# Stores behind row loads, a count of its own for the first norm, and row work moved into the first two experts

## The chip, the cores and the metric

The kernel runs on one core of one Trainium2 chip. The metric is device time in microseconds (us) of one launch; several executions are made and their median is compared. Engines: TensorE (PE in the views; PEld its weight loads), VectorE (DVE), ScalarE (ACT), GpSimd (POOL) and SyncE (SP), each with an instruction stream of its own. They are kept in order by semaphores: `then_inc` raises one, `wait_ge` holds an engine until it has a value. [...]

## The reference, cut to what matters

One transformer-like layer is applied to 128 prompt rows and to 256 sample rows (to which position rows are added), 1024 wide. A mixer (scans of three kinds, among them matrix-valued head states) is followed by a residual layer norm, a routed mixture of 16 experts and a second layer norm. The head states after the prompt are outputs too.

```python
y, finals = _mixer(x * (1 + sc1) + sh1, init, ...)
x = _layer_norm(ALPHA * x + g1 * y, ln1_g, ln1_b)
h = x * (1 + sc2) + sh2
scores = softmax(h @ w_router)            # 16 experts in 4 groups; best group, top 2 of it
act = silu(h @ w_gate[e]) * (h @ w_up[e]) * combine[e]
f = sum_e act @ w_down[e]
x = _layer_norm(ALPHA * x + g2 * f, ln2_g, ln2_b)
```

## The kernel before

The 384 rows are three row tiles (`NT` = 3) of 128 partitions. All matrices are held in float32; for a product, each operand is split in a rounded high part (ScalarE, `w_hi`) and a low part (VectorE subtracts, `w_lo`), and TensorE adds three products of them (`mm3`). A weight piece of 2 MB is split in four "units" of 128x1024; four unit buffers go round. SyncE streams the weight pieces.

**The mixer's end and the first norm.** TensorE projects with `w_out` in three parts; the third part is given out half row by half row, tile by tile (`y_ready`). In between `turned_rows(i)` transposes tile i's normed input and multiplies it with the router's weights. VectorE waits for the rows it needs, adds the position rows (L2048), then waits for the counts `ln_in` (eight loads: ln1_g, ln1_b, ln2_g, ln2_b, b_router, tri, desc16, iota) and `g_in` (four), folds the norm's gain and bias into the modulation rows (L2099 to L2102), and goes through `mixed_half(i, half)` (scale by g1, add to the residual, statistics; L2057 to L2059), `centred_rows`, `scaled_rows`, `router_logits`, `selection` and, at i == 2, `residual(0)`, which makes the row that the second norm will add to (L2091 to L2093: one small instruction and two of 1024 columns). Each uses `step`, which waits for the instruction's own end.

All loads of these rows are issued by POOL, in this order: after the last mask of the matrix heads it waits for `cfin_sb`, stores the final states `C_FIN` (512 KB) and `n_fin` (4 KB, in pieces of 4 bytes), loads the modulation rows (g1; then sc2 and sh2), the residual rows and the position rows, and then ln1_g, ln1_b, ln2_g, ln2_b, b_router, tri, desc16 and iota. Later come the indirect stores of the routed rows.

**Routing.** VectorE ranks the scores, TensorE counts ranks with `tri` (it too waits for `ln_in`), `slots_of(b)` makes selection matrices, and `selected(b)` multiplies the first two experts' rows out.

**The experts.** One expert has twelve units: up 4 to 7, the next expert's gate 8, 9, down 10 to 13, the next expert's gate 14, 15. TensorE runs 4 to 7, 8, the transposes of the activation (L1601), 9, 10 to 13, 14, 15, then turns the rows of the expert after next. VectorE makes the low parts in the same order, with `tokens_lo` before 8, `gated` (L2213) after 9 and `act_lo` (L2217) before 11. ScalarE makes the high parts, at most four units ahead of TensorE, with silu before 7. Before `expert(0)` VectorE runs `last_rows()`: residual(1), residual(2), `last_sel` (three instructions) and the picks (six small ones). TensorE transposes `last_sel` in its own `last_rows()` (L1571) between `expert(0)` and `expert(1)`. ScalarE's `last_rows()` stands behind its `expert(1)` and before `expert(2)`:

```python
def last_rows():                                   # ScalarE
    act.wait_ge(S["last_sel_T"], 1)
    act.activation(last_T, ps[:, 7, 0:T]..., ACT.Identity)           # L1046
    act.wait_ge(S["pick_ready"], 1)
    for c in range(2):
        for i in range(2):
            act.activation(pick_diag[:, c, i, :], ident, ...)       # L1050
...
expert(base + 1, p0, 1, p0 if base else None)
over = None
if base == 0:
    last_rows()
```

Of the kernel before, what the change touches and what calls it, by code (L numbers as in the profile page):

```python
# [29 lines left out]
ALU = mybir.AluOpType  # L30
# [3 lines left out]
P = 128  # L34
# [6 lines left out]
T = SEQ + LAT  # L41
NT = T // P
# [216 lines left out]
def build(nc, a, outs):  # L259
    with ExitStack() as ctx:  # L260
# [145 lines left out]
        def moe(off, n):  # L406
            return arena[:, off:off + n]
# [46 lines left out]
        ln_stats = early("ln_stats", 36).rearrange("p (i x) -> p i x", i=NT)  # L454
        ln_mv = early("ln_mv", 6).rearrange("p (i x) -> p i x", i=NT)
        ln_rstd, ln_rstd_a = [early(x, 3) for x in ("ln_rstd", "ln_rstd_a")]
        first_row = early("first_row", 16)
        SEL = [early(f"slot_sel{b}", 384).rearrange("p (i r) -> p i r", i=NT) for b in range(2)]

        kept = colsA  # L460
# [11 lines left out]
        row_sq = kept[:, 49:52]  # L472
        row_rstd = kept[:, 52:55]
        pick_diag = moe(6800, 512).rearrange("p (c i t) -> p c i t", c=2, i=2)
        last_sel = moe(7312, 384).rearrange("p (i r) -> p i r", i=NT)
# [187 lines left out]
        def _(pool):  # L663
# [53 lines left out]

            pool.wait_ge(S["cfin_sb"], 16)
            pool.dma_start(outs[4][0, 0].rearrange("d h p e -> p (d h) e"), C_FIN).then_inc(S["out_C"], 16)
            pool.dma_start(outs[5][0, 0].rearrange("d h p -> p (d h)"), n_fin, allow_slow_non_contiguous=True).then_inc(S["out_small"], 16)  # L720

            sem, value = TAKEN[("chan", "mo", C - 1)]
# [18 lines left out]
            for v, name in enumerate(("ln1_g", "ln1_b", "ln2_g", "ln2_b")):  # L741
                pool.dma_start(ln_b[:, v, :], a[name][0].partition_broadcast(P)).then_inc(S["ln_in"], 16)
            pool.dma_start(b_router, a["b_router"].partition_broadcast(P)).then_inc(S["ln_in"], 16)
            pool.dma_start(tri, a["consts"][:, 128:256]).then_inc(S["ln_in"], 16)
            pool.dma_start(desc16, a["consts"][:, 384:400]).then_inc(S["ln_in"], 16)
            pool.dma_start(iota, a["consts"][:, 256:384]).then_inc(S["ln_in"], 16)
            pool.wait_ge(S["zeroed_first"], 16 * ZERO_FIRST)
            pool.wait_ge(S["in_zeroed"], 16 * (12 - ZERO_FIRST))
# [422 lines left out]
        def _(pe):  # L1171
# [378 lines left out]
            pe.wait_ge(S["mask_ready"], 1)  # L1550
            pe.wait_ge(S["ln_in"], 16 * 8)
            mm(ps[:, 1, 0:64], tri, mask, True, False)
# [78 lines left out]
            def expert_pass(base):  # L1631
# [10 lines left out]
                if base:  # L1642
                    turn(base + 1, 1, p0)
                expert(base, 0, p0, True, base > 0)
                if base == 0:
                    last_rows()
                expert(base + 1, 1, p0, True)
                with pe.Fori(1, NPAIR - 1) as i:
# [35 lines left out]
        def _(dve):  # L1684
# [409 lines left out]

            dve.wait_ge(S["ln_in"], 16 * 8)
            dve.wait_ge(S["g_in"], 16 * 4)
            step(ts(first_row, desc16, -float(P), float(16 * P), ALU.mult, ALU.add))
            for s in range(2):
# [10 lines left out]
            centred_rows(0)  # L2109
            scaled_rows(0)  # L2110
            for i in range(1, NT):
                mixed_half(i, 0)
                router_logits(i - 1)
                selection(i - 1)
                if i == 2:
                    residual(0)
                mixed_half(i, 1)
                centred_rows(i)
                if i < NT - 1:
                    scaled_rows(i)  # L2120
# [61 lines left out]

            def last_rows():

                for i in (1, 2):
                    residual(i)
                for i in range(NT):
                    step(ts(last_sel[:, i, :], iota, last_rank[:, i:i + 1], last_w[:, i:i + 1], ALU.is_equal, ALU.mult), "last_sel")
                step(ts(in_last, rows, float((NE - 1) * P), None, ALU.is_ge))
                step(stt(in_last, rows, float(NE * P), in_last, ALU.is_lt, ALU.mult))  # L2190
                step(stt(rows, in_last, -float(P), rows, ALU.mult, ALU.add))
                step(dve.tensor_copy(row_e, rows))
                step(ts(in_last, in_last, -1.0, 1.0, ALU.mult, ALU.add))
                step(tt(pick_e.rearrange("p c i -> p (c i)"), pick_w.rearrange("p c i -> p (c i)"), in_last, ALU.mult), "pick_ready")
# [23 lines left out]

            def expert(n, b, bank=0):

# [9 lines left out]
                for q in range(1, 4):  # L2230
                    lo(n, 10 + q, down, q)
                for q in (2, 3):
                    lo(n, GATE_NEXT[q], gate, q)

            def expert_pass(base):
# [6 lines left out]
                lo(base, 3, gate, 3)  # L2242
                if base == 0:
                    last_rows()
                expert(base, 0, 0 if base else 5)
                over = dve.value_load(over_i[0:1, 0:1], min_val=0, max_val=T) if base == 0 else None
                expert(base + 1, 1)
                with dve.Fori(1, NPAIR - 1) as i:
                    for b in range(2):
                        expert(2 * i + (base + b), b)  # L2250
                expert(base + NE - 2, 0)
                n = base + NE - 1
# [98 lines left out]
```

## Time and profile before

| | |
|---|---|
| median of 3 runs | 752.32 us (751.73 to 752.75) |
| profiled execution, its own time | 752.86 us |
| its span, first to last instruction | 751.0 us |
| TensorE busy | 686.0 us, 91% |
| VectorE busy | 575.5 us, 77% |
| ScalarE busy | 433.0 us, 58% |
| mean granted TensorE clock | 0.961 |

Times in the rows are us from the span's start. The profiled execution lies 1.86 us over its span and 0.54 us over the median. The granted clock is a share of the full 2.4 GHz. In square brackets after an instruction stands the time its engine was idle before it and which instruction released it; L12 is line 12 of the kernel.

### The profile page before, as it was taken

To read this page: it belongs to the slowest core of one execution; us is meant where nothing else is said; L and a number is where in the kernel's file an instruction comes from. 1 tells how busy PE (TensorE), PEld (TensorE's weight loads), DVE (VectorE), ACT (ScalarE), POOL (GpSimd) and SP (SyncE) were. 2 spreads that over 40 slices of the span, in tenths; PEclk is the share of its full clock that TensorE was granted. 3 is DMA by queue.
4 is the path that set the end of the run, shared out by engine and by line. 5 is a ranking of instruction groups with operands and counts; after the bars stand their busy time and mean duration, and the time that the engine had idled before them with its cause. 6 is when DMAs were issued, how large, how long until landed. Compare 5 with 4: busy or idle time off the path is not lost.

```text
span 751.0 us, 12527 instructions
## 1 busy us (share of the span) xinstructions
PE 686.0 (91%) x4818; PEld 552.4 (74%) x4818; DVE 575.5 (77%) x838; ACT 433.0 (58%) x604; POOL 57.1 (8%) x88
## 2 busy tenths in 40 slices
PE   3599999999899999999794899999999999999881
PEld 2488988898689889944364878888888888888640
DVE  2649998788992457651767998998999998999765
ACT  1646966273223546530034378888888888888721
POOL 2060000000011001240000400000000000000210
PEclk9799999999999999999976999999999999999996
DMA  9999496466747898899403999999999999999242
GB/s 336 372 247 354 156 387 239 141 220 201 275 139 278 293 394 308 297 171 399 164 0 130 399 339 391 398 399 399 400 399 399 399 400 398 400 398 388 86 143 84
DMA packets 91508, 220.06 MB, mean 293 GB/s; under 512 B 3336, under 2 KB 3632, under 8 KB 91456
## 3 DMA queue, kind: packets, MB, share of 16 engines
q1 hardware_dynamic: 85200, 200.29, 72.1%
q0 software_dynamic: 5840, 18.94, 8.3%
q8 instruction: 33, 0.54, 0.3%
q10 hardware_dynamic: 415, 0.14, 0.1%
q14 instruction: 20, 0.16, 0.1%
HBM read 179.99 MB, written 39.36 MB: 292 GB/s over the span
## 4 chain that ended last, share of the span: by engine, by line
PE 69%; DVE 18%; DMA 6%; ACT 3%; issue 2%; SPq 1%; POOL 1%; DVEq 0%; ACTq 0%
PE ps L1173 66%; DMA iota<-in_consts 4%; DMA ring<-in_w_in 3%; PE ps L1582 2%; DVE w_lo L1745 2%; DVE arena L1900 1%; DVE arena L1899 1%; PE ps L1601 1%; DVE arena L1845 1%; DVE w_lo L2199 1%; ACT w_hi L829 1%; DVE arena L2093 1%; DVE arena L2290 1%; DVE arena L2092 1%; DVE arena L2292 1%
## 5 line engine op out<-in xcount | busy, mean ns | idle before, releaser
L2199 DVE TENSOR_TENSOR w_lo<-arena,w_hi 128x1024 fp32r<-128x1024 f32 x96 | 115.0, 1221 | 9.4 <-ACT w_hi L1057 8.3
L2199 DVE TENSOR_TENSOR w_lo<-ring,w_hi 128x1024 fp32r<-128x1024 f32 x92 | 109.9, 1221 | 8.8 <-ACT w_hi L1057 7.8
L1057 ACT ACTIVATE w_hi<-arena 128x1024 fp32r<-128x1024 f32 x96 | 101.2, 1064 | 17.0 <-PE ps L1173 16.8
L1173 PE MATMUL ps<-h_hi,w_lo 128*128 128x384 f32 x288 | 101.8, 354 | 7.4 <-DVE w_lo L1745 5.2
L1057 ACT ACTIVATE w_hi<-ring 128x1024 fp32r<-128x1024 f32 x92 | 96.8, 1063 | 19.8 <-PE ps L1173 19.5
L1173 PE MATMUL ps<-w_hi,slot_tokens_lo 128*128 128x512 f32 x256 | 103.1, 403 | 2.1 <-DVE w_lo L2199 2.1
L1173 PE MATMUL ps<-w_hi,slot_tokens_hi 128*128 128x512 f32 x256 | 101.0, 394 | 0.0
L1173 PE MATMUL ps<-w_lo,slot_tokens_hi 128*128 128x512 f32 x256 | 100.5, 393 | 0.0
L1173 PE MATMUL ps<-h_lo,w_hi 128*128 128x384 f32 x288 | 97.3, 338 | 0.0
L1173 PE MATMUL ps<-h_hi,w_hi 128*128 128x384 f32 x288 | 97.3, 338 | 0.0
L1745 DVE TENSOR_TENSOR w_lo<-ring,w_hi 128x1024 fp32r<-128x1024 f32 x44 | 53.7, 1225 | 23.6 <-ACT w_hi L829 22.6
L1173 PE MATMUL ps<-ring,arena 128*128 128x512 f32 x144 | 65.9, 616 | 0.4 <-DVE arena L1771 0.4
L829 ACT ACTIVATE w_hi<-ring 128x1024 fp32r<-128x1024 f32 x44 | 46.1, 1052 | 31.1 <-PE ps L1173 29.9
L1173 PEld LDWEIGHTS ps<-h_hi,w_lo 128*128 128x128 f32 x288 | 54.9, 191 | 12.3 <-issue 9.0
L1173 PE MATMUL ps<-arena 128*32 128x32 f32 (+5 forms) x1528 | 56.3, 220 | 4.1 <-DVE arena L1984 1.4
L1173 PEld LDWEIGHTS ps<-w_hi,slot_tokens_lo 128*128 128x128 f32 x256 | 48.6, 190 | 11.7 <-DVE w_lo L2199 2.5
L1173 PEld LDWEIGHTS ps<-w_hi,slot_tokens_hi 128*128 128x128 f32 x256 | 48.4, 189 | 10.4
L905 ACT ACTIVATE arena<-ps,small 128x384 f32<-128x384 f32 x32 | 18.5, 579 | 64.9 <-PE ps L1173 64.8
L1173 PEld LDWEIGHTS ps<-w_lo,slot_tokens_hi 128*128 128x128 f32 x256 | 48.6, 190 | 9.3
L1173 PEld LDWEIGHTS ps<-h_lo,w_hi 128*128 128x128 f32 x288 | 55.0, 191 | 0.6
L1173 PEld LDWEIGHTS ps<-h_hi,w_hi 128*128 128x128 f32 x288 | 54.8, 190 | 0.0
L1173 PEld LDWEIGHTS ps<-arena 128*32 128x32 f32 (+3 forms) x1528 | 44.4, 122 | 13.4 <-issue 5.7
(362 smaller groups left out, 1118.7 us busy)
## 6 DMA issues: line engine op xcount, KB each, us to landing
slot_rows<-arena SPq DMA_DIRECT2D x12, 2048.0 KB, 18.3
ring<-in_w_in SPq DMA_DIRECT2D x11, 2048.0 KB, 10.4
ring<-in_w_ada SPq DMA_DIRECT2D x10, 2048.0 KB, 9.0
ring<-in_w_up SPq DMA_DIRECT2D x8, 2048.0 KB, 15.0
ring<-in_w_down SPq DMA_DIRECT2D x8, 2048.0 KB, 11.2
arena<-in_w_gate SPq DMA_DIRECT2D x8, 2048.0 KB, 15.5
arena<-in_w_down SPq DMA_DIRECT2D x8, 2048.0 KB, 11.9
arena<-in_w_up SPq DMA_DIRECT2D x8, 2048.0 KB, 15.1
```

The source lines that it names most:

```text
L829: act.activation(part_unit(w_hi, u % 4, col), raw_unit(p % NSLOT, u % 4, col), ACT.Copy).then_inc(S["hi_ready"], 1)
L905: act.activation(chunk(dst_of[g], c), bank[:, 0:T], ACT.Gelu_apprx_tanh if g == "rg" else ACT.Identity, bias=bias).then_inc(S["z_taken"], 1)
L1057: act.activation(w_hi[:, at_ % 4, :], raw[:, q * QUARTER:(q + 1) * QUARTER], ACT.Copy).then_inc(S["hi_ready"], 1)
L1173: return pe.matmul(out, lhsT, rhs, start=start, stop=stop, skip_group_check=open_)
L1582: last = pe.transpose(ps[:, half, k * P:(k + 1) * P], XG[b][:, (4 * half + k) * P:(4 * half + k + 1) * P], ident)
L1601: last = pe.transpose(ps[:, 2, k * P:(k + 1) * P], AC[:, k * P:(k + 1) * P], ident)
L1745: tt(lo, raw, hi.bitcast(F32), ALU.subtract).then_inc(S["lo_dve"], 1)
L1845: step(dve.tensor_tensor_scan(hv, av, uv, init, ALU.mult, ALU.add))
L1899: step(tt(qh[right_q], qh[right_q], first.broadcast_to(shape), ALU.mult))
L1900: step(tt(kh[1 - right_q], kh[1 - right_q], last.broadcast_to(shape), ALU.mult))
L2092: step(stt(X1[:, i, :], X1[:, i, :], mean(i), gain, ALU.subtract, ALU.mult))
L2199: tt(w_lo[:, at_ % 4, :], raw[:, q * QUARTER:(q + 1) * QUARTER], w_hi[:, at_ % 4, :].bitcast(F32), ALU.subtract).then_inc(S["lo_dve"], 1)
```

## The change

- POOL: the wait for `cfin_sb` and the stores of `C_FIN` and `n_fin` move from ahead of the modulation rows to behind the load of iota.
- The loads of ln1_g and ln1_b are counted on `g_in` instead of `ln_in`. VectorE waits for `g_in` (six loads) ahead of the folding of gains, and for `ln_in` (now six) behind `scaled_rows(0)`, where `first_row` is now made. TensorE's wait for `ln_in` has the new count.
- `residual(0)` runs at i == 1 instead of i == 2.
- VectorE's `last_rows()` ahead of `expert(0)` is gone. `residual(1)` and `last_slots()` (the three `last_sel`) stand inside expert 0, and `residual(2)` and `picks()` inside expert 1, each behind unit 13 and ahead of unit 14. `value_load` of the overflow count moves behind the loop of experts.
- TensorE's `last_rows()` moves from behind `expert(0)` to behind `expert(1)`. ScalarE's stream is unchanged.
- `ln_mv`, `ln_rstd` and `ln_rstd_a` get places in `kept`, since they are now used inside the experts.

```diff
--- before.py
+++ after.py
@@ -452,8 +452,6 @@
         gain_c, bias_c = [early(x, 16).rearrange("p (k s) -> p k s", s=2) for x in ("gain_cols", "bias_cols")]
         least = early("least_win", 16)
         ln_stats = early("ln_stats", 36).rearrange("p (i x) -> p i x", i=NT)
-        ln_mv = early("ln_mv", 6).rearrange("p (i x) -> p i x", i=NT)
-        ln_rstd, ln_rstd_a = [early(x, 3) for x in ("ln_rstd", "ln_rstd_a")]
         first_row = early("first_row", 16)
         SEL = [early(f"slot_sel{b}", 384).rearrange("p (i r) -> p i r", i=NT) for b in range(2)]
 
@@ -471,6 +469,8 @@
         row_mean = kept[:, 46:49]
         row_sq = kept[:, 49:52]
         row_rstd = kept[:, 52:55]
+        ln_rstd, ln_rstd_a = kept[:, 55:58], kept[:, 58:61]
+        ln_mv = kept[:, 61:67].rearrange("p (i x) -> p i x", i=NT)
         pick_diag = moe(6800, 512).rearrange("p (c i t) -> p c i t", c=2, i=2)
         last_sel = moe(7312, 384).rearrange("p (i r) -> p i r", i=NT)
         last_T = moe(7696, 384).rearrange("p (i t) -> p i t", i=NT)
@@ -715,10 +715,6 @@
                                              pattern=[[0, nb], [sgn, P]], channel_multiplier=-sgn)
                     ins.then_inc(S["p_mask"], 1)
 
-            pool.wait_ge(S["cfin_sb"], 16)
-            pool.dma_start(outs[4][0, 0].rearrange("d h p e -> p (d h) e"), C_FIN).then_inc(S["out_C"], 16)
-            pool.dma_start(outs[5][0, 0].rearrange("d h p -> p (d h)"), n_fin, allow_slow_non_contiguous=True).then_inc(S["out_small"], 16)
-
             sem, value = TAKEN[("chan", "mo", C - 1)]
             pool.wait_ge(S[sem], value)
             pool.wait_ge(S["mod_stored"], 16)
@@ -739,11 +735,14 @@
             pool.dma_start(pos2, a["pos"].rearrange("(i p) d -> p i d", p=P)).then_inc(S["x2_in"], 16)
             pool.wait_ge(S["out_S"], 16)
             for v, name in enumerate(("ln1_g", "ln1_b", "ln2_g", "ln2_b")):
-                pool.dma_start(ln_b[:, v, :], a[name][0].partition_broadcast(P)).then_inc(S["ln_in"], 16)
+                pool.dma_start(ln_b[:, v, :], a[name][0].partition_broadcast(P)).then_inc(S["g_in" if v < 2 else "ln_in"], 16)
             pool.dma_start(b_router, a["b_router"].partition_broadcast(P)).then_inc(S["ln_in"], 16)
             pool.dma_start(tri, a["consts"][:, 128:256]).then_inc(S["ln_in"], 16)
             pool.dma_start(desc16, a["consts"][:, 384:400]).then_inc(S["ln_in"], 16)
             pool.dma_start(iota, a["consts"][:, 256:384]).then_inc(S["ln_in"], 16)
+            pool.wait_ge(S["cfin_sb"], 16)
+            pool.dma_start(outs[4][0, 0].rearrange("d h p e -> p (d h) e"), C_FIN).then_inc(S["out_C"], 16)
+            pool.dma_start(outs[5][0, 0].rearrange("d h p -> p (d h)"), n_fin, allow_slow_non_contiguous=True).then_inc(S["out_small"], 16)
             pool.wait_ge(S["zeroed_first"], 16 * ZERO_FIRST)
             pool.wait_ge(S["in_zeroed"], 16 * (12 - ZERO_FIRST))
             pool.wait_ge(S["route_ready"], 1)
@@ -1548,7 +1547,7 @@
             turned_rows(NT - 1)
 
             pe.wait_ge(S["mask_ready"], 1)
-            pe.wait_ge(S["ln_in"], 16 * 8)
+            pe.wait_ge(S["ln_in"], 16 * 6)
             mm(ps[:, 1, 0:64], tri, mask, True, False)
             for j in range(NT):
                 n = NT - j
@@ -1642,9 +1641,9 @@
                 if base:
                     turn(base + 1, 1, p0)
                 expert(base, 0, p0, True, base > 0)
+                expert(base + 1, 1, p0, True)
                 if base == 0:
                     last_rows()
-                expert(base + 1, 1, p0, True)
                 with pe.Fori(1, NPAIR - 1) as i:
                     for b in range(2):
                         expert(2 * i + (base + b), b, i + p0, True)
@@ -2092,9 +2091,7 @@
                 step(stt(X1[:, i, :], X1[:, i, :], mean(i), gain, ALU.subtract, ALU.mult))
                 step(stt(X1[:, i, :], X1[:, i, :], ln_rstd_a[:, i:i + 1], bias, ALU.mult, ALU.add))
 
-            dve.wait_ge(S["ln_in"], 16 * 8)
-            dve.wait_ge(S["g_in"], 16 * 4)
-            step(ts(first_row, desc16, -float(P), float(16 * P), ALU.mult, ALU.add))
+            dve.wait_ge(S["g_in"], 16 * 6)
             for s in range(2):
                 step(tt(H2[:, 0, :], bias, sc2_b[s], ALU.mult))
                 step(tt(sh2_b[s], sh2_b[s], H2[:, 0, :], ALU.add))
@@ -2108,11 +2105,13 @@
 
             centred_rows(0)
             scaled_rows(0)
+            dve.wait_ge(S["ln_in"], 16 * 6)
+            step(ts(first_row, desc16, -float(P), float(16 * P), ALU.mult, ALU.add))
             for i in range(1, NT):
                 mixed_half(i, 0)
                 router_logits(i - 1)
                 selection(i - 1)
-                if i == 2:
+                if i == 1:
                     residual(0)
                 mixed_half(i, 1)
                 centred_rows(i)
@@ -2180,12 +2179,12 @@
             step(tt(last_w, last_w, both_w, ALU.mult))
             slots_of(1)
 
-            def last_rows():
-
-                for i in (1, 2):
-                    residual(i)
+            def last_slots():
+
                 for i in range(NT):
                     step(ts(last_sel[:, i, :], iota, last_rank[:, i:i + 1], last_w[:, i:i + 1], ALU.is_equal, ALU.mult), "last_sel")
+            def picks():
+
                 step(ts(in_last, rows, float((NE - 1) * P), None, ALU.is_ge))
                 step(stt(in_last, rows, float(NE * P), in_last, ALU.is_lt, ALU.mult))
                 step(stt(rows, in_last, -float(P), rows, ALU.mult, ALU.add))
@@ -2216,7 +2215,7 @@
                 dve.wait_ge(S["act_T_sb"], n + 1)
                 tt(ACL, ps[:, 2, :].rearrange("p (k j) -> p k j", k=C), ACH.bitcast(F32), ALU.subtract).then_inc(S["act_lo"], 1)
 
-            def expert(n, b, bank=0):
+            def expert(n, b, bank=0, rows_of=None):
 
                 up, down, gate = expert_slot(1, b), expert_slot(2, b), expert_slot(0, 1 - b)
                 for q in range(4):
@@ -2229,6 +2228,12 @@
                 act_lo(n)
                 for q in range(1, 4):
                     lo(n, 10 + q, down, q)
+                if rows_of is not None:
+                    residual(rows_of)
+                if rows_of == 1:
+                    last_slots()
+                if rows_of == 2:
+                    picks()
                 for q in (2, 3):
                     lo(n, GATE_NEXT[q], gate, q)
 
@@ -2240,14 +2245,12 @@
                 lo(base, 2, gate, 2)
                 tokens_lo(base, 0, (1,))
                 lo(base, 3, gate, 3)
-                if base == 0:
-                    last_rows()
-                expert(base, 0, 0 if base else 5)
-                over = dve.value_load(over_i[0:1, 0:1], min_val=0, max_val=T) if base == 0 else None
-                expert(base + 1, 1)
+                expert(base, 0, 0 if base else 5, None if base else 1)
+                expert(base + 1, 1, 0, None if base else 2)
                 with dve.Fori(1, NPAIR - 1) as i:
                     for b in range(2):
                         expert(2 * i + (base + b), b)
+                over = dve.value_load(over_i[0:1, 0:1], min_val=0, max_val=T) if base == 0 else None
                 expert(base + NE - 2, 0)
                 n = base + NE - 1
                 up, down = expert_slot(1, 1), expert_slot(2, 1)
```

## Rows read from the trace of the kernel before

**Rows 1.** The page: chain by engine; costliest group (busy us, mean ns | idle).

```profile
PE 69%; DVE 18%; DMA 6%; ACT 3%; issue 2%; SPq 1%; POOL 1%; DVEq 0%; ACTq 0%
...
L2199 DVE TENSOR_TENSOR w_lo<-arena,w_hi 128x1024 fp32r<-128x1024 f32 x96 | 115.0, 1221 | 9.4 <-ACT w_hi L1057 8.3
```

**Rows 2.** The chain that ended last, in order of time: start, us, what.

```profile
333.95 27.17 DMA iota<-in_consts
...
397.65 0.70 DVE arena L2057
...
442.55 8.52 PE ps L1173 x36
...
460.96 8.52 PE ps L1173 x36
...
479.12 8.51 PE ps L1173 x36
```

**Rows 3.** Timeline of TensorE, 300 to 452: start, us, engine, line, operation, shapes.

```profile
328.36 34.50 PE L1173 MATMUL ps<-ring,arena 128*128 128x512 f32 x80
...
362.86 7.08 PE L1173 MATMUL ps<-ring,arena 128*128 128x512 f32 x16
...
388.71 1.04 PE L1529 MATMUL ps<-small,arena 128*128 128x128 f32 x8
...
391.80 3.68 PE L1173 MATMUL ps<-ring,arena 128*128 128x512 f32 x8
...
431.98 0.50 PE L1173 MATMUL ps<-w_hi,slot_tokens_lo 128*128 128x512 f32 x1 [2.10 <-DVE w_lo L2199]
...
440.53 0.60 PE L1601 MATMUL ps<-small,arena 128*128 128x128 f32 x4
...
451.77 0.49 PE L1571 MATMUL ps<-small,arena 128*128 128x128 f32 x3
```

**Rows 4.** Timeline of VectorE, 315 to 470.

```profile
353.73 2.29 DVE L2048 TENSOR_TENSOR arena<-arena 128x2048 f32<-128x2048 f32 x1 [20.69 <-DMA arena<-in_pos]
...
361.53 1.23 DVE L2099 TENSOR_TENSOR arena<-arena 128x1024 f32<-128x1024 f32 x1
...
369.81 0.69 DVE L2057 TENSOR_TENSOR arena<-ps,gain_rows 128x512 f32<-128x512 f32 x1
...
372.25 0.69 DVE L2057 TENSOR_TENSOR arena<-ps,gain_rows 128x512 f32<-128x512 f32 x1
...
385.55 0.69 DVE L2057 TENSOR_TENSOR arena<-ps,gain_rows 128x512 f32<-128x512 f32 x1 [4.07 <-PE ps L1173]
...
422.68 0.15 DVE L2091 TENSOR_SCALAR ln_rstd_a<-ln_rstd 128x1 f32<-128x1 f32 x1
...
428.33 1.11 DVE L2188 TENSOR_SCALAR arena<-iota,small 128x128 f32<-128x128 f32 x3
...
430.70 4.63 DVE L2199 TENSOR_TENSOR w_lo<-ring,w_hi 128x1024 fp32r<-128x1024 f32 x4
...
445.81 4.87 DVE L2199 TENSOR_TENSOR w_lo<-arena,w_hi 128x1024 fp32r<-128x1024 f32 x4
```

**Rows 5.** Timeline of ScalarE, 300 to 492.

```profile
431.43 1.05 ACT L1057 ACTIVATE w_hi<-ring 128x1024 fp32r<-128x1024 f32 x1
...
464.98 0.47 ACT L1046 ACTIVATE arena<-ps 128x384 f32<-128x384 f32 x1
...
466.52 2.94 ACT L1057 ACTIVATE w_hi<-ring 128x1024 fp32r<-128x1024 f32 x3
```

**Rows 6.** Stretch: PE, PEld, DVE, ACT, POOL busy; granted clock; DMA share; GB/s.

```profile
431.95:435.64 3.69, 3.66 (x10) 2.87 (x11) 3.69 (x4) 2.48 (x4) 0.00 (x0) 0.56 0.80 224
```

**Rows 7.** DMA: a stretch, columns as above; two issues, us to landing.

```profile
322.00:334.00 12.00, 12.00 (x32) 5.47 (x31) 7.87 (x20) 4.25 (x4) 5.68 (x11) 1.00 0.90 107
...
out<-small POOLq DMA_DIRECT2D x1, 4.0 KB, 15.3
...
arena<-in_ln_b POOLq DMA_DIRECT2D x1, 512.0 KB, 26.6
```

## Prediction, made before the changed kernel ran

> **What bounds the kernel now.** I read the chain of waits by engine first: TensorE holds 69% of it and VectorE 18% [rows 1], so an edit pays only where one of these two is last. Then the same chain in order of time. Two places answer to the change. The load of iota stands in it for 27.17 us, from 333.95 to 361.12 [rows 2]: that is the eight-load count at the head of the first norm. The second is the start of the experts: expert 0's up weights are multiplied from 431.98, after a wait of 2.10 us for VectorE [rows 3], and each expert then gives one "down" start, at 442.55, 460.96 and 479.12 [rows 2]. That is 18.16 us an expert. I call these starts D0, D1 and D2; they are my clock for the second half.
>
> TensorE does not wait while the load is awaited: 80 matmuls of the output projection take 34.50 us and the next 16, 7.08 us, so it is busy until 369.94 [rows 3]. VectorE finishes adding the position rows at 356.02, sits still, and prepares the gains from 361.53 to 369.81, 8.28 us [rows 4]. Its sums of row tile 0 then come too late for TensorE, whose next projections come too late for VectorE: it waits 4.07 us for them before 385.55 [rows 4].
>
> **Part 1, the first norm.** VectorE now waits for ln1_g and ln1_b alone. ln1_b was issued at 330.79 and took 26.6 us [rows 7], so it was there at 357.4; the 512 KB store of C_FIN and the store of n_fin (4-byte pieces) no longer lie ahead of it in POOL's queue. The six loads of the modulation rows, which POOL issued behind them, go out up to 3 us sooner too, and the position rows, whose addition ended at 356.02 [rows 4], come earlier with them. How much earlier it lands no row tells directly. From 322 to 334 the DMA engines were 90% busy and moved only 107 GB/s, and n_fin landed 15.3 us after its issue [rows 7]. If those two stores are what clogs them, the rows land about ten us earlier.
>
> By the Trainium skill ("DMA: Bandwidth & Descriptors", Anatomy of one DMA, SWDGE path) bytes cost their size over 436 GB/s, so that C_FIN would be worth only an estimated 1.2 us; the last landing would be 356.2, and the sum below would come out half a us longer. The 107 GB/s speak against it as the whole cost.
>
> The first half row of tile 0 needs the projection's first output (362.86), the second half row its second (362.86 plus half of 7.08, so 366.4) [rows 3]. With the gains ready by 362.9 (preparation begun by 354.6, which needs the position rows added by then) the first half starts at 362.86 and, 2.44 us long (369.81 to 372.25 [rows 4]), ends before the second output. A preparation begun as late as 355.5 loses nothing, since the second half starts with that output anyway. I take 366.45. From this half row (372.25) to the last tile's second half row (397.65) lie 25.40 us, of which 4.07 are the wait [rows 2, 4]. The instructions between stay the same (residual(0) only moves one tile up; first_row, 0.2 us, joins them): 21.5 us. TensorE keeps up: free at 369.94, turned rows and logits of a tile 3.1 us (388.71 to 391.80), two projections 7.1 us, thus 380.1, again 3.1 and 3.5: its last output stands at 386.8 [rows 3]. So the last half row starts at 388.0 instead of 397.65: **9.65 us gained**. Lower bound: ln1_b as before, at 357.5, gives 365.8, 368.2, 389.7: 7.9 us. Upper: the last output itself, 10.8 us. ln_in and tri, iota now have until 371 and 398, ten us and more beyond their landing. The C_FIN store is now issued at about 334.5, behind iota; SyncE's wait for it stands before expert 1's gate weights, which go out at about 400 (with h2_ready, 410 less the 9.65), and POOL's own next work, the indirect stores, comes later still. So I price it at nothing; 60 us late, it would hold those weights back.
>
> The new places of ln_mv and ln_rstd change no duration; I price them at nothing.
>
> **Part 2, expert 0.** Before, VectorE does residual(1), residual(2), last_sel and the picks in one piece from 422.68 to 430.70, 8.02 us, and only then unit 4 [rows 4]. TensorE waits for it until 431.98 [rows 3] and then runs 3.69 us at a granted clock of 0.56 [rows 6], that is mostly at 1.2 GHz instead of 2.4, which costs 3.69 x 0.44 = 1.6 us. With this piece gone the next things are late: ScalarE writes unit 7's high part only from 431.43, after its table load [rows 5], so VectorE's unit 7, a subtraction of 1.22 us [rows 1], ends at 433.7, the tokens' low halves at 434.9, unit 8 at 436.1, unit 9 and the gating product at 437.85. The transposes follow, and from their start to D0 it is 440.53 to 442.55, 2.02 us [rows 2, 3]. D0 = 439.9: **2.65 us gained**, not the 3.85 of wait and clock. Bounds: 1.6 (if the small waits now drop the clock) and 3.85.
>
> **Part 3, the two blocks.** After unit 13 of expert 0 VectorE now does residual(1) and last_sel, 8.02 halved: by 428.33 the two residuals had taken 5.65, so a residual is 2.82; last_sel is 1.15, the picks 1.22 [rows 4]. The blocks are 3.97 and 4.05 us. Before, unit 14 is begun by VectorE at 445.81, D0 + 3.26 [rows 4]. Now it ends at D0 + 3.26 + 3.97 + 1.22 + 0.05 = D0 + 8.5. TensorE wants it when its 24 down matmuls are through, D0 + 5.6 (36 matmuls take 8.52 [rows 2]). It stands still 2.9 us in expert 0 and, by the same sum, 3.0 in expert 1. Neither is short beside the 2.1 us before 431.98, after which the clock fell [rows 3, 6]: 1.6 us more each. Bounds for each clock term: 0 and 1.6.
>
> **Part 4, last_rows of TensorE behind expert 1.** ScalarE's place for it has not moved: after the high parts of expert 1, before expert 2. Before, TensorE's three transposes were at 451.77 [rows 3], 13 us ahead of ScalarE, which copies at 464.98 and goes on to expert 2's high parts at 466.52 without a wait, 1.54 us [rows 5]. Now the transposes start 9.22 us after the down start (442.55 to 451.77 [rows 2, 3]) plus the 3.0 of the block. Queued behind ScalarE's wait is unit 4 of expert 2, and TensorE and VectorE both wait for it. From the transposes' start: 0.55 to ScalarE, 1.54, high part 1.06, low part 1.22, handovers 0.1: 4.5, of which 0.25 is the transposes' own: **4.2 us** idle. Then all four buffers are empty and ScalarE and VectorE feed expert 2 as they go, with silu, the token copies and the out rows in between; as in part 2, unit 8 and the gating product come late, 1.3 us in all (bounds 0 and 2). Here the slow clock hides inside the same waits, so it costs about nothing more. VectorE's register load, now behind the loop, I price at nothing: it waits for no other engine there.
>
> **Sum.** Experts: -2.65 + 2.9 + 1.6 + 3.0 + 1.6 + 4.2 + 1.3 = +11.95. Norm: -9.65. Net +2.3 us. The profiled execution took 752.86 us with a span of 751.0, 1.86 around it, and lies 0.54 over the median, so 755.2 for it and **754.6** for the median. Behind D2 nothing is left over: each engine finds its old distance again, at TensorE's pace.
>
> **Rivals.** (a) The clock holds in one of the two idles (+0.7, 753.0) or in both (-0.9, 751.4). For: the handover gaps of an ordinary expert leave it at 1.0; against: 2.1 us sufficed before. (b) Rows do not land earlier, and the change does in part 1 only half of what it says: +1.75, 756.3. For: the queue's other seven loads stay; against: 107 GB/s. (c) Faster: VectorE's slack hides the two blocks. It decides at unit 14 of expert 0: a block of up to 5.6 - 3.26 - 1.28 = 1.1 us would be free, one of 3.97 is not. The price is 2.9 + 3.0 + 3.2, and the time 745.5. For: twelve low parts in sequence take some 14 us (four take 4.63 [rows 4]), which, with 2.6 us of small ones, leaves a good us of an expert's 18.16 free; against: that is all they leave. (d) Faster by less: the clock also holds at tile 2 of the norm and in both idles; some 0.8 more than (a), 750.6.
>
> **Chances and range.** Forecast 0.50, (a) 0.19 for one and 0.11 for both, (b) 0.08, (c) 0.05, (d) 0.07. This kernel's measurement tells 0.2%, 1.5 us, from nothing. Slower: the forecast less 0.03 for its lower edge, and (b): 0.55. Same: (a) and that 0.03, 0.33. Faster: (c) and (d), 0.12. The range runs from (d) to (b), 750.8 to 756.4.
>
> **What would show it.** Right: the last half row's L2057 about ten us before its old place; unit 4 right behind unit 3; TensorE idle for 3 us before unit 14 of experts 0 and 1, released by VectorE, with a clock near 0.5 behind it; ScalarE's L1046 waiting some 7 us for TensorE's transposes, and TensorE waiting 4 us before expert 2. Wrong: no hole before unit 14, or a hole of ScalarE under 4 us, or VectorE still waiting in the norm.

## The result and the profile after

The changed kernel takes 755.45 us (median of 7 runs, 753.81 to 756.17) against 751.73 us for the kernel before (7 runs, 748.08 to 753.61): a ratio of 1.0049, 95% interval 1.0026 to 1.0071. It is slower by 3.7 us, half a percent, with an interval of 2.0 to 5.3. The profiled execution took 754.52 us with a span of 752.7, at a mean granted clock of 0.963. In this kernel most line numbers are lower by one: L1172 is L1173 of before, L2056 is L2057.

The chain by engine, from its page, where iota's load is gone from the share of DMA [rows 1]:

```profile
PE 73%; DVE 16%; ACT 4%; DMA 3%; issue 2%; SPq 1%; DVEq 0%; ACTq 0%
```

DMA issues of the changed kernel (KB of one, us from issue to landing). The load of ln1_b took 26.6 us before [rows 7]; the two stores are now behind iota:

```profile
arena<-in_ln_b POOLq DMA_DIRECT2D x1, 512.0 KB, 9.9
...
out<-arena POOLq DMA_DIRECT2D x1, 512.0 KB, 19.1
...
out<-small POOLq DMA_DIRECT2D x1, 4.0 KB, 18.4
```

VectorE's timeline, changed kernel. The gains are prepared 22 us earlier than at 361.53 [rows 4], and VectorE then sits still until TensorE's output arrives:

```profile
339.29 1.23 DVE L2096 TENSOR_TENSOR arena<-arena 128x1024 f32<-128x1024 f32 x1 [0.29 <-DMA arena<-in_ln_b]
...
361.40 0.69 DVE L2056 TENSOR_TENSOR arena<-ps,gain_rows 128x512 f32<-128x512 f32 x1 [13.86 <-PE ps L1172]
...
387.90 0.69 DVE L2056 TENSOR_TENSOR arena<-ps,gain_rows 128x512 f32<-128x512 f32 x1 [1.31 <-PE ps L1172]
```

TensorE's timeline there: the third tile's eight projection matmuls took 3.68 us before [rows 3].

```profile
361.30 7.08 PE L1172 MATMUL ps<-ring,arena 128*128 128x512 f32 x16
...
382.58 5.21 PE L1172 MATMUL ps<-ring,arena 128*128 128x512 f32 x8
...
414.16 0.48 PE L1172 MATMUL ps<-w_hi,slot_tokens_lo 128*128 128x512 f32 x1
...
429.92 0.50 PE L1172 MATMUL ps<-w_hi,expert_act_lo 128*128 128x512 f32 x1
```

The last half row starts at 387.90 instead of 397.65 and unit 0 of expert 0 at 414.16 instead of 424.14. Of these 9.75 and 9.98 us, 1.56 are no gain of the change: this execution reached the run of 80 projection matmuls at 326.80, before it was 328.36 [rows 3]; it was as far ahead at 301.4 already, where nothing has changed. D0 is 429.92, another 2.65 earlier than unit 0.

The chain in order of time, through the two blocks and the stop of ScalarE, to D2:

```profile
437.15 1.23 DVE w_lo L2198
...
438.43 3.02 PE ps L1172 x12
...
458.30 1.24 DVE w_lo L2198
...
459.58 4.49 PE ps L1172 x12
464.07 0.99 PE ps L1581 x8
465.06 0.34 PE ps L1570 x3
...
465.43 0.49 ACT arena L1045
...
468.06 1.24 DVE w_lo L2198
...
469.34 9.50 PE ps L1172 x30
...
480.76 8.49 PE ps L1172 x36
```

Stretches (us; PE, PEld, DVE, ACT, POOL busy; granted clock; DMA share; GB/s): tile 2's projection, the hole before unit 14 of expert 0 and the twelve matmuls behind it, unit 14 of expert 1 with the turned rows, and two pieces of the refill of expert 2:

```profile
382.00:384.00 2.00, 2.00 (x8) 1.39 (x8) 1.93 (x3) 0.35 (x1) 0.00 (x0) 0.57 0.00 0
435.40:438.40 3.00, 0.30 (x2) 0.00 (x0) 2.86 (x6) 1.14 (x2) 0.00 (x0) 1.00 1.03 410
438.40:441.50 3.10, 3.07 (x14) 2.52 (x15) 3.10 (x3) 1.08 (x2) 0.00 (x0) 1.00 1.03 415
459.55:465.00 5.45, 5.42 (x21) 4.38 (x22) 1.11 (x1) 0.00 (x0) 0.00 (x0) 0.69 0.98 360
469.30:472.60 3.30, 3.26 (x8) 2.62 (x9) 3.30 (x3) 3.25 (x6) 0.00 (x0) 0.50 0.00 0
472.60:475.00 2.40, 2.40 (x8) 1.91 (x7) 2.40 (x4) 2.06 (x4) 0.00 (x0) 0.62 0.40 82
```

Waits (who waits for whom: sum in us, times, longest). Behind ScalarE's wait stands expert 2's unit 4, whose high part starts only at 466.98:

```profile
ACT arena L1045 <- PE ps L1570: 10.3, 1, 10.3
PE ps L1172 <- DVE w_lo L2198: 10.2, 4, 3.9
```

The reader is to see one sum in this. Up to D0 the changed kernel is 12.63 us ahead (442.55 to 429.92). From D0 to D1 (451.00, TensorE's first down matmul of expert 1) it needs 21.08 us instead of 18.41 [rows 2], from D1 to D2 29.76 instead of 18.16. Expert 1 to 2 alone gives 11.6 us away: 2.98 of standing before unit 14 (459.58, less 451.00 and 5.6), 1.59 of slower matmuls (4.49 + 0.99 against 3.02 + 0.87 at full clock), 4.28 from last_rows' transposes at 465.06 to 469.34, and 2.67 in the thirty matmuls of the refill (9.50; at full clock the same thirty take 6.83). Of these thirty the first twelve account for 2.2 (469.34 to 474.54, 5.20 us against the 3.02 of twelve at full clock). D2 is 1.64 us later than before, and from there to the end both kernels take 271.9 us.

In the changed kernel `last_sel` lies over 384 columns of the bias row that `residual(2)` reads afterwards in expert 1, so tile 2's residual row has other values there; instructions and durations don't depend on it. This holds for x1_experts_only and s1_act_rows_late too, not for the other experiments.

### The profile page after: what moved, and what is told of

Read it like the earlier page. It is cut to its first block, busy times and chain, and to the rows that moved or that the text cites. A ratio compares the mean times of both kernels' runs of the same rounds, so it can differ in the third digit from the quotient of the medians.

```text
span 752.7 us, 12528 instructions
## 1 busy us (share of the span) xinstructions
PE 684.7 (91%) x4818; PEld 549.7 (73%) x4818; DVE 575.1 (76%) x838; ACT 432.8 (58%) x604; POOL 56.9 (8%) x88
## 4 chain that ended last, share of the span: by engine, by line
PE 73%; DVE 16%; ACT 4%; DMA 3%; issue 2%; SPq 1%; DVEq 0%; ACTq 0%
PE ps L1172 70%; DMA ring<-in_w_in 3%; DVE w_lo L2198 2%; PE ps L1581 2%; DVE w_lo L1744 2%; DVE arena L1899 1%; DVE arena L1898 1%; DVE arena L1844 1%; PE ps L1600 1%; ACT w_hi L828 1%; ACT w_hi L1056 1%; SPq L547 1%; DVE arena L2091 1%; DVE arena L2092 1%; DVE arena L2293 1%
## 5 line engine op out<-in xcount | busy, mean ns | idle before, releaser
L1172 PE MATMUL ps<-w_hi,slot_tokens_lo 128*128 128x512 f32 x256 | 104.4, 408 | 10.2 <-DVE w_lo L2198 10.2
L1172 PE MATMUL ps<-h_hi,w_lo 128*128 128x384 f32 x288 | 101.5, 352 | 6.8 <-DVE w_lo L1744 5.2
L1172 PE MATMUL ps<-w_hi,slot_tokens_hi 128*128 128x512 f32 x256 | 101.8, 398 | 0.0
L1172 PE MATMUL ps<-w_lo,slot_tokens_hi 128*128 128x512 f32 x256 | 101.3, 396 | 0.0
L1172 PE MATMUL ps<-h_hi,w_hi 128*128 128x384 f32 x288 | 97.3, 338 | 0.0
L1172 PE MATMUL ps<-h_lo,w_hi 128*128 128x384 f32 x288 | 97.2, 337 | 0.0
L1172 PE MATMUL ps<-ring,arena 128*128 128x512 f32 x144 | 64.6, 606 | 0.4 <-DVE arena L1770 0.4
L1172 PEld LDWEIGHTS ps<-w_hi,slot_tokens_lo 128*128 128x128 f32 x256 | 49.0, 192 | 21.2 <-DVE w_lo L2198 10.8
L1172 PEld LDWEIGHTS ps<-h_hi,w_lo 128*128 128x128 f32 x288 | 54.5, 189 | 11.7 <-issue 8.5
L1172 PE MATMUL ps<-arena 128*32 128x32 f32 (+5 forms) x1528 | 55.3, 219 | 4.2 <-DVE arena L1900 1.4
L1172 PEld LDWEIGHTS ps<-w_hi,slot_tokens_hi 128*128 128x128 f32 x256 | 48.9, 191 | 10.7
L1172 PEld LDWEIGHTS ps<-w_lo,slot_tokens_hi 128*128 128x128 f32 x256 | 49.1, 192 | 9.4
L1172 PEld LDWEIGHTS ps<-h_lo,w_hi 128*128 128x128 f32 x288 | 54.7, 190 | 0.5
L904 ACT ACTIVATE arena<-ps,small 128x384 f32<-128x384 f32 x32 | 18.6, 580 | 62.8 <-PE ps L1172 62.8
L1172 PEld LDWEIGHTS ps<-h_hi,w_hi 128*128 128x128 f32 x288 | 54.6, 190 | 0.0
L1172 PE MATMUL ps<-w_hi,expert_act_lo 128*128 128x512 f32 x128 | 51.8, 405 | 2.6 <-DVE expert_act_lo L2216 1.4
## 6 DMA issues: line engine op xcount, KB each, us to landing
ring<-in_w_in SPq DMA_DIRECT2D x11, 2048.0 KB, 10.3
```

Source lines behind the costliest of these rows:

```text
L904: act.activation(chunk(dst_of[g], c), bank[:, 0:T], ACT.Gelu_apprx_tanh if g == "rg" else ACT.Identity, bias=bias).then_inc(S["z_taken"], 1)
L1172: return pe.matmul(out, lhsT, rhs, start=start, stop=stop, skip_group_check=open_)
```

## The experiments

Three theories stood against each other. A, the forecast's own: the norm part gains 8 to 10 us, and the blocks and ScalarE's stop lose 11 to 12. B: the moved stores cost time somewhere later. C: the parts only work together. The experiments form two groups, each with runs of the kernel before of its own. First group: kernel before 750.37 us (17 runs, 746.50 to 754.14).

A profile shows one execution, and it need not lie at the median: that of n1 took 738.16 us (median 740.39), that of x1 760.25 (762.95), that of s1 749.46, the slowest of its twelve, and that of d1 737.23, the fastest of its eight. The start of the run of 80 projection matmuls alone lies between 325.66 and 329.48 in the ten profiles. Where two profiles are compared below, times are therefore counted from an event in the same trace.

### n1_norm_only: the norm part alone

The three store lines behind iota, the counts and `residual(0)` as changed; the experts as in the kernel before.

```diff
             for i in range(1, NT):
                 ...
-                if i == 2:
+                if i == 1:
                     residual(0)
...
             def last_rows():
                 for i in (1, 2):
                     residual(i)
```

> The first norm's part of the change alone (stores behind iota, own count for ln1_g and ln1_b, residual(0) at i == 1); the experts as before. Theory A (the norm gains, the blocks in the experts and ScalarE's stop give more than that back): 8 to 10 us faster than before, 742 to 744 where before has 752; VectorE runs its gains long before TensorE's first output, and expert 0 starts about 10 us earlier, still with TensorE's wait of 2.1 us for the residual rows. Theory B (the moved stores clog the DMA engines later, from 342 to 354 in the changed kernel, and that is what costs): not faster by more than 3 us. Theory C (the parts are worth what they are only together): under 5 us.

Measured: 740.39 us (6 runs, 737.57 to 744.24), ratio 0.9875 (0.9839 to 0.9910). TensorE's timeline and one stretch, right behind the wait before unit 4:

```profile
382.25 3.68 PE L1172 MATMUL ps<-ring,arena 128*128 128x512 f32 x8
...
419.80 0.50 PE L1172 MATMUL ps<-w_hi,slot_tokens_lo 128*128 128x512 f32 x1 [1.70 <-DVE w_lo L2198]
```

```profile
419.80:421.80 2.00, 2.00 (x9) 1.65 (x10) 2.00 (x2) 2.00 (x4) 0.00 (x0) 1.00 0.97 264
```

The norm part gains about 9.4 us alone (0.0125 of 750.37; 6.8 to 12.1 by the interval), so C falls. With the stores in their new place nothing later becomes slower: from D2 to the end this kernel takes 270.4 us, the kernel before 271.9. So B falls. VectorE's last half row starts at 386.46, without a wait, since tile 2's projection kept the full clock here (3.68 us against 5.21 in the changed kernel, for the same code). The wait before unit 4 was 1.70 us, and the clock stayed at 1.00 behind it; before, it was 2.10 us and the clock fell [rows 3, 6]. That is some 2 us of gain which this kernel has and the changed one can't add, since there the experts' part takes the wait away.

### x1_experts_only: the experts' part alone

```diff
-                if i == 1:
+                if i == 2:
                     residual(0)
...
-            dve.wait_ge(S["g_in"], 16 * 6)
+            dve.wait_ge(S["ln_in"], 16 * 8)
+            dve.wait_ge(S["g_in"], 16 * 4)
```

and the stores back ahead of the modulation rows; the experts as changed.

> The experts' part alone (residual(1) and last_sel in expert 0, residual(2) and picks in expert 1, TensorE's last_rows behind expert 1); the first norm as before. Theory A: 10 to 13 us slower than before, 762 to 765: TensorE still 3 us before unit 14 of experts 0 and 1 and 4 us ahead of expert 2. Theory B: within 3 us of before. In this kernel, as in the changed one, last_sel is written over columns 144 to 527 of the bias row that residual(2) still reads.

Measured: 762.95 us (6 runs, 758.30 to 764.38), ratio 1.0158 (1.0124 to 1.0191). The chain in order of time:

```profile
444.51 4.61 PE ps L1173 x12
449.12 0.87 PE ps L1582 x8
...
467.25 3.02 PE ps L1173 x12
```

The experts' part costs 11.9 us (0.0158 of 750.37), inside the expected 10 to 13. The two ratios multiplied give 1.0031 (0.9961 to 1.0099 from the ends of the intervals); the whole change has 1.0049. Within that noise the parts add up, as A has it. An overlap of some 2 us, as at the wait before unit 4, would not be seen in these intervals. Here the clock fell behind the first block (4.61 us for its twelve matmuls) and held behind the second (3.02); in the changed kernel it was the other way round.

### s1_act_rows_late: the changed kernel, ScalarE's last_rows behind its expert 2

```diff
                 over = None
+                expert(base + 2, p0 + 1, 0, p0 if base else None)
                 if base == 0:
                     last_rows()
                     act.wait_ge(S["route_ready"], 2)
                     over = act.value_load(over_i[0:1, 0:1], min_val=0, max_val=T)
-                expert(base + 2, p0 + 1, 0, p0 if base else None)
```

> The changed kernel with ScalarE's last_rows (and its register load) behind its expert 2 instead of ahead of it. It takes ScalarE's stop away and leaves both blocks. Theory A, with the price of the stop at 4.2 us of TensorE's idle and 1.3 to 2.5 in expert 2: 5.5 to 7 us faster than the changed kernel, 748.5 to 750 where that has 755.4, so 2 to 3.5 us faster than before. If the stop were hidden and the blocks were the whole loss: within 1 us of the changed kernel.

Measured: 747.43 us (12 runs, 744.20 to 749.46), ratio 0.9954 (0.9934 to 0.9975). The chain of waits:

```profile
460.83 4.60 PE ps L1172 x12
465.43 0.87 PE ps L1581 x8
466.30 0.33 PE ps L1570 x3
466.63 6.84 PE ps L1172 x30
...
475.40 8.51 PE ps L1172 x36
```

Both blocks and one drop of the clock are still there (the other block's twelve matmuls, at 439.68, took 3.02 us), but the transposes are followed by expert 2 at once, and its thirty matmuls take 6.84 us. From the first selection matmul to D2 are 73.05 us here (402.35 to 475.40) and 79.81 in the changed kernel (400.95 to 480.76): 6.8 us less. The medians differ by 8.0 us, the ratios by 0.0095 or 7.1 us. That is slightly more than the expected 5.5 to 7. More than half of the net loss of the experts' part (11.9) hangs on one call of ScalarE that the change did not touch; the register load behind it moved along and was not tried by itself.

### d1_residuals_ahead: the two blocks shortened

`residual(1)` and `residual(2)` ahead of expert 0, in VectorE's idle time there; only `last_sel` (1.1 us) and the picks (1.2 us) inside the experts; TensorE's last_rows behind expert 0 again.

```diff
-                if rows_of is not None:
-                    residual(rows_of)
...
+                if base == 0:
+                    residual(1)
+                    residual(2)
                 expert(base, 0, 0 if base else 5, None if base else 1)
...
                 expert(base, 0, p0, True, base > 0)
-                expert(base + 1, 1, p0, True)
                 if base == 0:
                     last_rows()
+                expert(base + 1, 1, p0, True)
```

> The changed kernel with residual(1) and residual(2) ahead of expert 0 again, last_sel alone in expert 0 and the picks alone in expert 1 (1.15 and 1.22 us, each behind unit 13), and TensorE's last_rows behind expert 0 again. The changed trace shows VectorE idle for 4.94 us ahead of unit 4, and unit 4's low part is wanted only at the end of unit 3, so 5.65 us of residuals should be free there, and blocks of 1.1 to 1.2 us just hidden at unit 14. Theory A: no wait of TensorE above 0.5 us at unit 4 and unit 14, 10 to 12 us faster than before, 740 to 742. If even a block of 1.2 us costs its length: 2.5 us less gain.

Measured: 741.06 us (8 runs, 737.23 to 741.76), ratio 0.9875 (0.9849 to 0.9901). The chain shows no VectorE between the down starts any more:

```profile
427.83 8.68 PE ps L1172 x36
436.51 0.87 PE ps L1581 x8
437.39 0.33 PE ps L1570 x3
437.71 6.85 PE ps L1172 x30
...
446.41 8.78 PE ps L1172 x36
```

Blocks of 1.1 and 1.2 us cost next to nothing: D0 to D1 is 18.58 us (18.41 before), D1 to D2 18.42 (18.16). Its median lies in the expected 740 to 742, its gain of 9.4 us (0.0125) just short of the expected 10 to 12. Against n1_norm_only nothing can be told apart, though TensorE's wait for VectorE ahead of unit 4 is gone: in n1's profile that wait was 1.7 us and had left the clock up, so there was little to win. In d1's own profile the clock fell at tile 2 of the norm (5.38 us for the eight matmuls).

### The stores taken apart

Second group: kernel before 751.62 us (11 runs, 750.17 to 753.89). All three have the norm part's counts and `residual(0)`; the two stores stand where the table says.

```diff
+            pool.wait_ge(S["cfin_sb"], 16)
+            pool.dma_start(outs[4][0, 0]..., C_FIN).then_inc(S["out_C"], 16)
...
-            pool.wait_ge(S["cfin_sb"], 16)
-            pool.dma_start(outs[4][0, 0]..., C_FIN).then_inc(S["out_C"], 16)
             pool.dma_start(outs[5][0, 0]..., n_fin, ...).then_inc(S["out_small"], 16)
```

(the core of g2_only_small_behind against n1_norm_only)

> The first norm's counts and residual(0) at i == 1, with both stores of the states left where they were, ahead of all row loads; experts as before. Theory A (the stores clog the queue, and the count alone lets VectorE go when ln1_b is there, at about 357.4): VectorE's gains begin at 357 to 358 instead of 361.5 and the last half row comes 7 to 8 us earlier, so 7 to 8 us faster than before, 1 to 2 us short of the norm part as a whole. Rival (the moved stores are what pays): under 4 us.

> The norm part with only n_fin (1024 pieces of 4 bytes) behind iota and the 512 KB store of C_FIN left ahead of the row loads. If n_fin's small pieces clog the DMA engines: ln1_b lands 10 to 12 us after its issue, near 340. If C_FIN does: it lands 25 us or more after its issue, near 355, and the slow stretch stays at 322 to 334. Time: as the norm part as a whole in the first case (9 to 10 us under before), up to 1.5 us more in the second.

> The norm part with only C_FIN behind iota and n_fin left ahead of the row loads: the mirror of the run before. If n_fin clogs: ln1_b lands about 25 us after its issue. If C_FIN clogs: 10 to 12 us, and the slow stretch moves behind iota, to about 342 to 354.

| | C_FIN | n_fin | ln1_b lands after | VectorE's gains begin | us (median, range) | ratio |
|---|---|---|---|---|---|---|
| g1 | ahead | ahead | 27.6 | 358.82 | 743.75 (738.79 to 745.24) | 0.9883 (0.9857 to 0.9909) |
| g3 | behind | ahead | 22.0 | 352.01 | 741.68 (741.40 to 745.88) | 0.9885 (0.9857 to 0.9913) |
| g2 | ahead | behind | 15.1 | 346.08 | 739.90 (737.78 to 741.10) | 0.9834 (0.9812 to 0.9855) |
| n1 | behind | behind | 10.8 | 340.24 | 740.39 (737.57 to 744.24) | 0.9875 (0.9839 to 0.9910) |

Stretches of g1 with both stores ahead, and of g2, where n_fin was issued at 335.1 instead of about 318 (columns as above):

```profile
326.00:330.00 4.00, 4.00 (x13) 1.88 (x12) 3.44 (x7) 0.30 (x1) 1.68 (x3) 1.00 1.03 46
330.00:334.00 4.00, 4.00 (x11) 1.77 (x10) 2.49 (x11) 0.00 (x0) 4.00 (x9) 1.00 0.76 62
```

```profile
330.00:334.00 4.00, 4.00 (x10) 1.73 (x10) 2.99 (x14) 0.00 (x0) 3.84 (x7) 1.00 0.99 343
350.00:354.00 4.00, 4.00 (x11) 1.85 (x10) 3.90 (x4) 0.00 (x0) 0.00 (x0) 1.00 0.93 136
354.00:358.00 4.00, 4.00 (x11) 1.76 (x10) 0.33 (x1) 0.00 (x0) 0.00 (x0) 1.00 0.42 84
```

The slow stretch goes where n_fin goes: 46 and 62 GB/s with it ahead, 343 GB/s at the same place without it, and 136 and 84 GB/s at the place to which it went (the 84 at a DMA share of only 0.42, when less was left to move). In g3, with n_fin alone ahead, it is 79 GB/s at 322 to 326. Moving n_fin alone brings ln1_b 12.5 us earlier (27.6 to 15.1), C_FIN alone 5.6 us (27.6 to 22.0). That lies between the two things expected of g2 and g3: both stores hold the loads up, n_fin more. For the time it hardly matters: the half rows wait for TensorE's projection, so gains that begin at 340, 346 or 352 are all in time. Counted from the start of the 80 matmuls, the last half row comes after 59.8 us in g2 and n1 and after 61.1 in g3, where tile 2's eight matmuls ran into a fallen clock (5.27 us); before it was 69.3. Only the gains of g1, from 358.8, come late: 62.8 us. It still keeps 7.9 us of the gain by its median (8.8 by its ratio), as the forecast's lower bound of 7.9 has it for rows that land as before. The larger part of the norm's gain thus comes from the count that no longer waits for six further loads, and from `residual(0)` moved; the two weren't tried apart.

### d2_residuals_spread: the work where the slack is

As d1, but `residual(0)` and `residual(1)` ahead of expert 0, the two long instructions of `residual(2)` one behind unit 13 and one behind unit 15 of expert 0, `last_sel` and the picks behind units 13 and 15 of expert 1, TensorE's last_rows behind expert 1, ScalarE's as in s1.

```diff
+                if base == 0:
+                    residual(0)
+                    residual(1)
...
                 if rows_of == 1:
-                    last_slots()
+                    residual(2, second=False)
                 if rows_of == 2:
-                    picks()
+                    last_slots()
                 for q in (2, 3):
                     lo(n, GATE_NEXT[q], gate, q)
+                if rows_of == 1:
+                    residual(2, first=False)
+                if rows_of == 2:
+                    picks()
```

> From the version with residual(1) and residual(2) ahead of expert 0, residual(0) is taken out of the norm too: residual(0) and residual(1) ahead of expert 0, the two long instructions of residual(2) in expert 0 (one behind unit 13, one behind unit 15), last_sel behind unit 13 and the picks behind unit 15 of expert 1, TensorE's last_rows behind expert 1 and ScalarE's behind its expert 2. Theory A (only VectorE work beyond 1.1 us at unit 14, or 2.4 us by the next unit 4, costs anything, and the norm is bound by VectorE): 1.5 to 3 us faster than the version with two residuals ahead, 738 to 740. If the norm is bound by TensorE once residual(0) is gone: under 1 us.

Measured: 737.47 us (5 runs, 736.73 to 738.49), ratio 0.9815 (0.9797 to 0.9832), the fastest of all kernels here, 1.85% under the kernel before. VectorE's timeline in expert 0, and TensorE's unit 14 there:

```profile
429.42 1.28 DVE L2092 SCALAR_TENSOR_TENSOR arena<-arena,small 128x1024 f32<-128x1024 f32 x1
430.74 2.36 DVE L2198 TENSOR_TENSOR w_lo<-arena,w_hi 128x1024 fp32r<-128x1024 f32 x2
433.02 1.28 DVE L2094 SCALAR_TENSOR_TENSOR arena<-arena,small 128x1024 f32<-128x1024 f32 x1
...
432.02 0.50 PE L1172 MATMUL ps<-w_hi,slot_tokens_lo 128*128 128x512 f32 x1 [0.27 <-DVE w_lo L2198]
```

In pieces of 1.3 us the same work leaves TensorE a wait of 0.27 us before unit 14 in place of 2.73. From D0 to D2 it is 38.18 us here (425.98 to 464.16), 37.00 in d1, 36.57 before and 50.84 in the changed kernel: spreading costs 1.6 us in the experts, the blocks and the stop, with the clock, cost 14.3. Beside g2, which has the row work in the old place and is at 0.9834 (0.9812 to 0.9855), the intervals overlap, so spreading this work is not shown to be worth anything by itself. What is shown is that it can be moved with little of the loss.

## Why the prediction was right, and where its terms were off

The forecast was 754.6 us, +2.3 us; measured were 755.45 and +3.7. The mechanism held in the main: the norm's gain, both blocks and ScalarE's stop are where the forecast put them. One step was wrong, that the slow clock would cost nothing in expert 2's refill, and one of the forecast's own signs of being wrong showed, VectorE still waiting in the norm. That the sum came out near is in part luck.

- **Norm, -9.65.** As the records stand -9.75, but without the earlier mixer -8.2, so the term was 1.5 too large. VectorE's wait did not vanish but was 1.31 us at tile 2, because the clock had fallen over TensorE's eight matmuls (0.57 from 382 to 384; 5.21 us instead of 3.68). The working had taken 3.5 us for these eight, a row at full clock. In n1, where the clock held, the last half row comes 9.45 us earlier, counted from the start of the 80 matmuls. Rival (b) falls: ln1_b landed after 9.9 us instead of 26.6.
- **Expert 0, -2.65.** Measured -2.65: unit 0 gained 9.98, D0 12.63. The lateness named as next in line was there: unit 7's low part starts at 422.51, ScalarE's high part just before it, and TensorE waits 0.76 us for VectorE before unit 8. (The bound of 3.85 for "wait and clock" is a little more than the rows give, 2.10 + 1.6 = 3.7.)
- **Block in expert 0, +2.9 and +1.6.** The wait was as forecast, unit 14 at D0 + 8.51 (forecast D0 + 8.5). The clock term was 0: 1.00 in the hole and behind it, as rival (a) has it for one of the two idles.
- **Block in expert 1, +3.0 and +1.6.** Measured 2.98 and 1.59.
- **ScalarE's stop, +4.2.** 4.28 with the transposes that used to stand in the expert before (0.25), so 4.0. ScalarE waited 10.3 us for them, where the forecast had some 7. s1 shows that it is this stop: moved away, 7 to 8 us come back.
- **Expert 2's refill, +1.3, and "the slow clock hides inside the same waits".** This sentence was wrong. At a granted clock of 0.50 to 0.62 the thirty matmuls took 9.50 us, 2.67 more than at full clock, and TensorE stood busy all through them: VectorE kept up, so there were no waits for the clock to hide in, and little of the lateness of unit 8. The upper bound of 2 was too low.
- **The sum.** Experts: -2.65 + 2.67 (D0 to D1) + 11.60 (D1 to D2) = +11.6; forecast +11.95. One clock drop less (1.6) and a dearer refill (1.4) cancel, which is luck. The experts' part alone measured +11.9. With the norm at -8.4 (unit 0, without the earlier mixer) the sum is +3.2, against +3.7 by the medians. Rival (a), one idle with its clock kept, is what happened in the profiled execution; its 753.0 was missed only because the norm gained less and the refill cost more.
- **Rival (c), slack hides the blocks**, fell at the place named for it: 1.1 and 1.2 us cost next to nothing (d1), 3.97 and 4.04 are not. **Rival (d)** fell with (a): one of three places kept its clock. Its extra 0.8 us had no ground either, since the sum had tile 2's matmuls at full clock already; and the range, 750.8 to 756.4, is not quite that of the rivals it names, 750.6 and 756.3.

The Trainium skill ("DMA: Bandwidth & Descriptors", Anatomy of one DMA, SWDGE path) prices bytes at their size over 436 GB/s. The trace comes near that while the loads are being moved (all of the core's DMA engines together: 412 GB/s from 330 to 334 and 391 from 338 to 342 in the changed kernel), and disagrees where n_fin's 4 KB in 4-byte pieces are: 183 GB/s from 342 to 346, at a DMA share of 1.29.

What stays open: why the clock fell in one hole and not in the other. Behind idle stretches of TensorE of some 3 us before unit 14 it held three times and fell three times: held in expert 0 and fell in expert 1 in the changed kernel and in s1, the other way round in x1. Before unit 4 it held behind 1.34 to 1.70 us (n1, g1, g2, g3) and fell behind 2.10. These are single executions, and no run here controls it.

## What to carry to other kernels

Before an instruction with a cross-engine wait stays put while its producer moves, count how late the producer now is and what stands queued behind the waiting instruction: an unchanged line cost about as much here (some 7 us) as both visible blocks together (2.9 and 3.0, and 1.6 for the clock). Work for an engine's slack goes in pieces no longer than the slack between two hand-overs (here pieces of 1.1 to 1.3 us cost 0.4 us in two experts in d1 and 1.6 in d2), not in a block as long as an expert's total. And a wait on a shared count is a wait on its slowest load; give the operands that are needed first a count of their own, and put stores of small pieces behind the loads.

## What the runs showed of the hardware

- A 4 KB store in pieces of 4 bytes (n_fin) holds up the transfers around it more than a 512 KB store: with it in the queue 46 and 62 GB/s at a DMA share of 1.03 and 0.76, without it 343; it took 13 to 21 us to land in all orders tried, and a 512 KB load behind it landed 12.5 us later than without (g1 against g2), against 5.6 us later for the 512 KB store (g1 against g3).
- The granted clock after a short idle is not settled by the code: the same eight projection matmuls took 5.21 us in the changed kernel (5.27 in g3, 5.38 in d1) and 3.68 in n1 (and in g2 and s1), after the same 1.13 us wait for ScalarE and the same sixteen narrow matmuls.
